# The triangular inverse on two diagonal 64x64 blocks, with part of its transposes on VectorE

## What is computed

```python
a_mat = jnp.einsum('bhncd,bhnsd->bhncs', kb, k) * decay * strict
m_mat = jnp.eye(chunk, dtype=jnp.float32) + a_mat
rhs = jnp.concatenate([vb, kb * jnp.exp(gc)[..., None]], axis=-1)
sol = lax.linalg.triangular_solve(m_mat, rhs, left_side=True, lower=True, unit_diagonal=True)
u_c, w_c = sol[..., :DV], sol[..., DV:]
```

## Time and profile before

| | |
|---|---|
| time, median of 3 runs | 1202.3 us (1195.59, 1203.81, 1202.3) |
| profiled execution, span | 1200.4 us |
| TensorE busy | 1187.7 us (99%) |
| VectorE busy | 790.3 us (66%) |
| ScalarE busy | 523.0 us (44%) |
| DMA | 99.69 MB, mean 83 GB/s |
| mean granted TensorE clock | 0.993 |

### The profile page before, as it was taken

One profiled execution on the slowest core, in us unless ns is written; L12 is line 12 of the kernel. 1 busy time (PEld: TensorE's weight loads), 2 busy tenths in 40 slices (PEclk: granted clock), 3 DMA queues, 4 the chain that ended last, 5 costly groups with the idle time before them and its releaser, 6 DMA issues.

```text
span 1200.4 us, 20994 instructions
## 1 busy us (share of the span) xinstructions
PE 1187.7 (99%) x8792; PEld 1162.9 (97%) x8792; DVE 790.3 (66%) x1153; ACT 523.0 (44%) x841; POOL 63.3 (5%) x48
## 2 busy tenths in 40 slices
PE   9999999999999999999999999999999999999997
PEld 9999999999999998999999897999999999999997
DVE  6887565767566733766665787547776667675764
ACT  6445343435345532433553454443354344354355
POOL 0000000000000300000104100220000000000003
PEclk9999999999999999999998999999999999999999
DMA  5322212222212332152300002422133121223112
GB/s 191 129 85 75 105 63 97 89 98 78 106 72 106 106 106 70 55 71 71 111 1 2 1 1 88 132 77 83 54 126 120 63 97 63 97 106 106 71 71 79
DMA packets 39213, 99.69 MB, mean 83 GB/s; under 512 B 12112, under 2 KB 15568, under 8 KB 39120
## 3 DMA queue, kind: packets, MB, share of 16 engines
q1 hardware_dynamic: 38064, 96.00, 24.0%
q10 hardware_dynamic: 1056, 2.36, 0.5%
HBM read 92.91 MB, written 5.44 MB: 82 GB/s over the span
## 4 chain that ended last, share of the span: by engine, by line
PE 95%; DVE 2%; ACT 1%; issue 1%; POOLq 0%; DVEq 0%; POOL 0%
PE ps L857 34%; PE ps L824 21%; PE ps L773 20%; PE ps L969 11%; PE ps L1361 4%; PE ps L737 1%; PE ps L1167 1%; PE ps L1375 1%; ACT x_hi L1443 1%; DVE w_lo L1950 1%; DVE h L2012 1%; PE ps L928 0%; PE ps L939 0%; PE ps L993 0%; PE ps L1273 0%
## 5 line engine op out<-in xcount | busy, mean ns | idle before, releaser
L857 PE MATMUL ps<-x_hi,s_hi 128*128 128x296 f32 (+1 forms) x576 | 171.5, 298 | 0.2
L857 PE MATMUL ps<-x_hi,s_lo 128*128 128x296 f32 (+1 forms) x576 | 171.0, 297 | 0.0
L857 PE MATMUL ps<-x_lo,s_hi 128*128 128x296 f32 (+1 forms) x576 | 170.7, 296 | 0.0
L773 PE MATMUL ps<-x_hi,w_hi 128*128 128x296 f32 (+1 forms) x608 | 135.8, 304 | 0.2 <-DVE x_lo L1955 0.2
L773 PE MATMUL ps<-x_lo,w_hi 128*128 128x296 f32 (+1 forms) x608 | 132.0, 298 | 0.0
L773 PE MATMUL ps<-x_hi,w_lo 128*128 128x296 f32 (+1 forms) x608 | 131.8, 298 | 0.0
L857 PE MATMUL ps<-t_hi,s_hi 128*128 128x296 f32 (+1 forms) x432 | 128.5, 297 | 0.0
L857 PE MATMUL ps<-t_hi,s_lo 128*128 128x296 f32 (+1 forms) x432 | 128.3, 297 | 0.0
L857 PE MATMUL ps<-t_lo,s_hi 128*128 128x296 f32 (+1 forms) x432 | 128.1, 296 | 0.0
L2049 DVE TENSOR_TENSOR s_lo<-s_sum,s_hi 128x1024 fp32r<-128x1024 f32 x72 | 88.2, 1225 | 44.1 <-ACT s_hi L1430 41.4
L857 PEld LDWEIGHTS ps<-x_hi,s_hi 128*128 128x128 f32 x576 | 108.5, 188 | 0.6 <-issue 0.6
(11 more groups left out here) (325 smaller groups left out, 2554.8 us busy)
## 6 DMA issues: line engine op xcount, KB each, us to landing
raw<-weights SPq DMA_DIRECT2D x150, 512.0 KB, 3.4
raw<-weights SPq DMA_DIRECT2D x16, 384.0 KB, 3.5
S<-states SPq DMA_DIRECT2D x1, 2048.0 KB, 10.5
new_state<-S ACTq DMA_DIRECT2D x1, 2048.0 KB, 6.8
y_t<-h SPq DMA_DIRECT2D x4, 336.0 KB, 2.3
h<-x_t SPq DMA_DIRECT2D x4, 296.0 KB, 4.6
h<-x_t SPq DMA_DIRECT2D x2, 592.0 KB, 7.4
raw<-weights SPq DMA_DIRECT2D x4, 256.0 KB, 5.2
```

Source lines behind the costliest of these rows:

```text
L773: last = nc.tensor.matmul(ps[:, slot if out is None else out, half, 0:w_half], w[:, slot, k, :], x[:, k, a:a + w_half], start=(k == 0 and ...
L857: last = nc.tensor.matmul(out, w[:, k, :], x[:, k, :], start=(start and k == 0 and r == 0), stop=(k == KT // 2 - 1 and r == 2), skip_group ...
```

## The change

For tiles 1 to 4 the levels 1 to 5 never leave the two 64x64 blocks on the diagonal. The change holds just these two blocks, one in partitions 0 to 63 and one in partitions 64 to 127, side by side in 64 columns (`x_small`, `y_small` in plane 0, `t_small`). A product of 128x128 becomes two of 64x64: rows 0 to 63 into partitions 0 to 63, and rows 64 to 127 into partitions 64 to 127 (`DIAGONAL`). VectorE's masks and subtractions of these levels have half the columns. Up to level 4 the blocks to be turned are 32x32 or smaller, so for the levels 0 to 4 X is made from Y by VectorE's own transpose of 32x32 blocks (`V.transpose`), and TensorE's transposes and ScalarE's copies of these levels are gone. After level 5, TensorE turns one 64x64 block per head and ScalarE copies it; the subtraction of level 5 is two instructions that write into the full Y. The subtraction of level 6 becomes a multiplication by -1. A wait of the old first transposes (`att_ready`, `y_ready`, `u_ready`) moves to `low` of level 1, q = 1. Tile 0 keeps its steps. The mask table is 128 columns narrower. `ORDER` is unchanged. The core of the diff:

```diff
@@ -244,10 +245,13 @@
 MASK = {}
 _at = 0
 for _n, _w in (("ident", P), ("incl", P), ("neg", P), ("incl4", P), ("neg4", P), ("same4", P),
-               ("levels", 7 * P), ("group", NG)):
+               ("levels", 4 * MAIN), ("ident64", HALF_P), ("levels64", 6 * HALF_P), ("group", NG)):
+
+DIAGONAL = (slice(0, HALF_P), slice(HALF_P, P))
...
@@ -263,11 +267,17 @@
     m[:, MASK["incl4"]] = (s <= c) & same
     m[:, MASK["neg4"]] = np.where((s <= c) & same, 0.0, -1e30)
     m[:, MASK["same4"]] = same
-    for l in range(7):
+    for l in range(6):
         w = 1 << l
-        a = MASK["levels"].start + l * P
         block = (s // (2 * w) == c // (2 * w)) & (s % (2 * w) < w) & (c % (2 * w) >= w)
-        m[:, a:a + P] = block.T if l else block
+        block = block.T if l else block
+        if l < 4:
+            a = MASK["levels"].start + l * MAIN
+            m[:, a:a + MAIN] = block[:, 0:MAIN]
+        a = MASK["levels64"].start + l * HALF_P
+        for r in DIAGONAL:
+            m[r, a:a + HALF_P] = block[r, r]
+    m[:, MASK["ident64"]] = s % HALF_P == c[:, 0:HALF_P]
...
@@ -484,6 +494,29 @@
         def half_bank(j, half, n):
             return bank(j).rearrange("p (x h c) -> p x h c", x=2, h=2)[0:n, half, :, 0:n]
 
+        def half_small(j, half):
+            return bank(j).rearrange("p (x h c) -> p x h c", x=2, h=2)[:, half, :, 0:HALF_P]
+
+        def x_small(t):
+            return XY[t % 2][:, 0, :, 0:HALF_P]
+
+        def y_small(t):
+            return XY[t % 2][:, 0, :, HALF_P:P]
+
+        def t_small(t):
+            return T1[t % 2][:, :, 0:HALF_P]
+
+        def two_heads(ap, q):
+            return ap[:, 2 * q:2 * q + 2]
+
+        def first_mask(l):
+            a = MASK["levels"].start + l * MAIN
+            return mask[0:MAIN, a:a + MAIN]
+
+        def small_mask(l):
+            a = MASK["levels64"].start + l * HALF_P
+            return mask[:, a:a + HALF_P]
...
@@ -1146,17 +1179,12 @@
                     for hd in range(H):
                         last = mm(heads(a, n)[0:n, hd, :], kv[:, hd, cols], kv[:, hd, cols])
                     last.then_inc(s["kk_ps"], 1)
-                else:
+                elif t == 0:
 
                     pe.wait_ge(s["y_first"][p], t // 2 + 1)
                     for q in range(2):
                         if q == 1:
-                            if t < 2:
-                                pe.wait_ge(s["att_ready"], t + 1)
-                            elif t == 2:
-                                pe.wait_ge(s["y_ready"][0][1], LEVELS[0] - 1)
-                            else:
-                                pe.wait_ge(s["u_ready"], t - 2)
+                            pe.wait_ge(s["att_ready"], t + 1)
                         turned(t, q)
 
             def turned(t, q):
@@ -1164,7 +1192,11 @@
                 n = TILES[t][1]
                 p, a, b, base = chain_at(t)
                 for hd in range(2):
-                    last = nc.tensor.transpose(half_bank(a + q, 0, n)[:, hd, :], inverse(t)[:, 2 * q + hd, 0:n], m("ident", n))
+                    if t == 0:
+                        last = nc.tensor.transpose(half_bank(a + q, 0, n)[:, hd, :], inverse(t)[:, 2 * q + hd, 0:n], m("ident", n))
+                    else:
+                        r = DIAGONAL[0]
+                        last = nc.tensor.transpose(half_small(a + q, 0)[r, hd, :], inverse(t)[r, 2 * q + hd, r], ident[r, r])
                 last.then_inc(s["x_ps"][p][q], 1)
             def low(t, lq):
@@ -1173,10 +1205,20 @@
                 n = TILES[t][1]
                 p, a, b, base = chain_at(t)
                 pe.wait_ge(s["x_ready"][p][q], base + l)
+                if t and l == 1 and q == 1:
+                    if t == 1:
+                        pe.wait_ge(s["att_ready"], t + 1)
+                    elif t == 2:
+                        pe.wait_ge(s["y_ready"][0][1], LEVELS[0] - 1)
+                    else:
+                        pe.wait_ge(s["u_ready"], t - 2)
                 for hd in range(2 * q, 2 * q + 2):
                     if l == 6:
                         last = mm(half_bank(a + q, 0, n)[HALF_P:P, hd - 2 * q, 0:HALF_P], AT[p][0:HALF_P, hd, HALF_P:P],
                                   XY[p][0:HALF_P, 0, hd, 0:HALF_P])
+                    elif t:
+                        for r in DIAGONAL:
+                            last = mm(half_small(a + q, 0)[r, hd - 2 * q, :], AT[p][r, hd, r], x_small(t)[r, hd, :])
                     else:
                         last = mm(half_bank(a + q, 0, n)[:, hd - 2 * q, :], AT[p][0:n, hd, 0:n], XY[p][0:n, 0, hd, 0:n])
                 last.then_inc(s["t1_ps"][p][q], 1)
@@ -1191,6 +1233,9 @@
                     if l == 6:
                         last = mm(half_bank(a + q, 1, n)[0:HALF_P, hd - 2 * q, HALF_P:P], T1[p][HALF_P:P, hd, 0:HALF_P],
                                   inverse(t)[HALF_P:P, hd, HALF_P:P])
+                    elif t:
+                        for r in DIAGONAL:
+                            last = mm(half_small(a + q, 1)[r, hd - 2 * q, :], t_small(t)[r, hd, :], y_small(t)[r, hd, :])
                     else:
                         last = mm(half_bank(a + q, 1, n)[:, hd - 2 * q, :], T1[p][0:n, hd, 0:n], inverse(t)[:, hd, 0:n])
                 last.then_inc(s["p_ps"][p][q], 1)
@@ -1199,6 +1244,8 @@
 
                 l, q = lq
                 p, a, b, base = chain_at(t)
+                if t and l < 5:
+                    return
                 pe.wait_ge(s["y_ready"][p][q], base + l)
                 turned(t, q)
...
@@ -1778,18 +1825,23 @@
             def start(t, i):
                 n = TILES[t][1]
                 p, a, b, base = chain_at(t)
-                if i == 1:
+                if i == 1 and t == 0:
                     for q in range(2):
                         turned(t, 0, q)
 
             def turned(t, l, q):
                 n = TILES[t][1]
                 p, a, b, base = chain_at(t)
-                act.wait_ge(s["x_ps"][p][q], base + l + 1)
-                nc.scalar.copy(pair(XY[p][:, 0], q, n), half_bank(a + q, 0, n)).then_inc(s["x_ready"][p][q], 1)
+                act.wait_ge(s["x_ps"][p][q], l + 1 if t == 0 else FLIPS[t])
+                if t:
+                    r = DIAGONAL[0]
+                    nc.scalar.copy(two_heads(x_small(t), q)[r], half_small(a + q, 0)[r]).then_inc(s["x_ready"][p][q], 1)
+                else:
+                    nc.scalar.copy(pair(XY[p][:, 0], q, n), half_bank(a + q, 0, n)).then_inc(s["x_ready"][p][q], 1)
 
             def flip(t, lq):
-                turned(t, *lq)
+                if t == 0 or lq[0] == 5:
+                    turned(t, *lq)
...
@@ -2456,19 +2508,46 @@
                 n = TILES[t][1]
                 p, a, b, base = chain_at(t)
                 if i:
+                    if t:
+                        for q in range(2):
+                            turned(t, 0, q)
                     return
                 dve.wait_ge(s["kk_ps"], t + 1)
                 dve.wait_ge(s["e_ready"], t + 1)
                 V.tensor_tensor(AT[p][0:n, :, 0:n], heads(a, n)[0:n], E_[p][0:n, :, 0:n], ALU.mult).then_inc(s["at_ready"], 1)
                 dve.wait_ge(s["at_ready"], t + 1)
 
-                link(V.tensor_tensor(T1[p][0:n, :, 0:n], AT[p][0:n, :, 0:n], over_heads(m("levels", n, 0), n), ALU.mult))
+                if t:
+                    for r in DIAGONAL:
+                        last = V.tensor_tensor(t_small(t)[r], AT[p][r, :, r], small_mask(0)[r].unsqueeze(1).to_broadcast([HALF_P, H, HALF_P]),
+                                               ALU.mult)
+                    link(last)
+                else:
+                    link(V.tensor_tensor(T1[p][0:n, :, 0:n], AT[p][0:n, :, 0:n], over_heads(first_mask(0), n), ALU.mult))
                 if t == 2:
                     dve.wait_ge(s["neg_vn_ps"], 1)
                 if t > 2:
                     dve.wait_ge(s["u_ps"], t - 2)
-                V.tensor_tensor(inverse(t)[:, :, 0:n], over_heads(m("ident", n), n), T1[p][0:n, :, 0:n],
-                                ALU.subtract).then_inc(s["y_first"][p], 1)
+                if t == 1 or t == 2:
+                    V.memset(inverse(t)[HALF_P:P, :, 0:HALF_P], 0.0)
+                if t:
+                    V.tensor_tensor(y_small(t), over_heads(mask[:, MASK["ident64"]], P), t_small(t),
+                                    ALU.subtract).then_inc(s["y_first"][p], 1)
+                else:
+                    V.tensor_tensor(inverse(t)[:, :, 0:n], over_heads(m("ident", n), n), T1[p][0:n, :, 0:n],
+                                    ALU.subtract).then_inc(s["y_first"][p], 1)
+
+            def turned(t, l, q):
+                p, a, b, base = chain_at(t)
+                if l == 0:
+                    dve.wait_ge(s["y_first"][p], t // 2 + 1)
+                else:
+                    dve.wait_ge(s["y_ready"][p][q], base + l)
```

(21 more changed lines are left out.)

3 lines of the change are left out of this document (2 added, 1 removed).

## The result

| | before | after |
|---|---|---|
| time, median (range) of 22 runs each | 1201.9 us (1195.55 to 1203.91) | 1205.72 us (1202.02 to 1211.84) |
| after over before, 95% interval | | 1.005 (1.0035 to 1.0065) |
| span of the profiled execution | 1200.4 us | 1203.9 us |
| mean granted clock of that execution | 0.993 | 0.982 |

The change makes the kernel 0.5% slower, under the 1% that I called the limit of what a measurement tells; the forecast was 0.9% faster.

The account below looks back on a forecast made before the run. TensorE was taken as the bound (95% of the span), VectorE next. Of 21.7 us off TensorE's list, 15.4 could count at best; less 4.4 for waits, gain 11: span 1189.4, median 1191 us, 8-in-10 range 1184 to 1206.

Parts of the forecast that it names:

- TensorE's list: TensorE's work in the gated-delta stage: 46.2 us of records go, 24.5 come, so 21.7 us shorter.
- The price of a pair: Two 64x64 block records on TensorE, run side by side, cost 0.0575 us together; 320 pairs make 18.4 us.
- The rival of blocks that do not overlap: In long runs each 64x64 record costs 0.0575 us; TensorE's list only 3.3 us shorter, 1198 to 1201; chance 0.15.
- VectorE's sum over the stage: Masks and subtractions get shorter, 40 transposes add 11.2 us: +3 us used, bounds -4 and +9.
- The rival of dear transposes: VectorE's transposes cost double, 0.56 us: 11 us more, VectorE the bound everywhere, gain 4, 1198; chance 0.08.
- Meshing: From 640 to 740 us both in-order engines, over 80% full, would not mesh perfectly: 4.4 us charged, 1 per 20.
- the bound by the fuller engine: Larger of TensorE's and VectorE's busy time per stretch, 640 to 740 us: 85.6 us, at most 14.4 gained there.
- The place was the one named: At the scan's step, state updates and an output operation precede two transposes: a new 1.5 us wait, up to three times.
- The clock: Granted clock, half speed from 626 to 640 us before the change; no added half clock was charged in the forecast.
- an extension: Half clock lasting past 640 us: without a slower kernel chance 0.07, slower by over 1% chance 0.10.
- held on to 660 us: Clock rival's case of half clock lasting from 626 to 660 us: costs up to 10 us, no gain, 1202.
- the good half: Part of the forecast 1186 to 1197 counted as under 1190.3, faster by over 1%: 0.23 of its chance 0.43.

Follow-up runs that it names:

- e3: Changed kernel, 16-column state products of the last two of four heads streamed wider; median 1205.4 us, ratio 1.005; its profiled execution was among three at 1196.2 to 1198.6.
- e2: Kernel before, with its 16-column state products streamed over all columns from the group's first to the tile's 80th; 1195.6 us, ratio 0.9968.
- e9: e5 with the first product (low) of every level 1 to 5 of tiles 1 to 4 streamed over 128 columns; 1192.2 us, ratio 0.9943.
- e5: Changed kernel with state products widened and each VectorE transpose put directly behind the subtraction that makes its Y; 1194.8 us, ratio 0.9957.
- e10: e8 with VectorE's transposes put back at the flip's own later place in the order; 1196.6 us, ratio 0.9974.
- e8: e5 with the first product (low) of tile 1 and of tile 2's levels 1 and 2 streamed over 128 columns; 1190.5 us, ratio 0.9921.

## Why the prediction was wrong, step by step

**TensorE's list: right, 2 us short.** Between before and the profiled e3, at the same clock in the stage, TensorE's busy time falls from 133.73 to 113.90, 19.8 us; the sum said 21.7. Between e2 and e9, both at full clock, it falls by 10.9, and the 160 wider pairs of e9 were put at 8 us: 18.9. The price of a pair holds over long runs. From e5, at full clock, in order of time:

```profile
708.21 0.68 PE L1002 MATMUL ps<-d_inv,d_t 64*64 64x64 f32 x16
708.73 0.63 PE L1002 MATMUL ps<-d_inv,d_a_t 64*64 64x64 f32 x16
```

Sixteen records, eight pairs, in 0.52 us: 0.065 a pair: the first pair of a run takes 0.05 more, the others the 0.0575 of the sum. The rival of blocks that do not overlap is out. The Trainium skill (TensorE: Matmul & The Clock Gate, What happens when you issue a matmul) gives about 62 ns per matmul where the sequencer's software decodes it. By the rows it is 0.52 / 16 = 0.033 us per record here, so that figure does not hold for this kernel. The Trainium skill (TensorEngine Tiling, Restrictions and Gotchas) says that a column-tiled array has no transpose mode for fp32 input. Here the 16 transposes of 64x64 blocks at L1199 are 16 records, not the 32 of full products; whether the array was column-tiled for them, no run tells.

**VectorE: prices right, sum 4 us too high.** By form, 600 to 780 us of after:

```profile
L2546 DVE STREAM_TRANSPOSE d_inv<-d_inv 128x128 f32<-128x128 f32 x40 | 10.8, 292 | 0.1
L2561 DVE TENSOR_TENSOR d_t<-ps,mask 128x128 f32<-128x128 f32 x40 | 10.7, 284 | 8.1 <-PE ps L1002 7.8
```

A transpose takes 292 ns (0.28 taken), a mask 284 (0.28). VectorE's sum over the stage goes from 100.71 to 99.64, where I had +3, well within the bounds. The rival of dear transposes is out.

**Meshing (how far both engines stay busy at once): the right mechanism, mis-sized.** I charged 4.4 us for it, on top of the bound by the fuller engine. Taken together, 21.7 us off the list and 11 off the time meant 10.7 us more of idle TensorE. In e3 against before it is 16.96 - 3.13 = 13.8 us, and the stage is 6.0 us shorter, not 11. The missing 5 us are 3.1 of idle time and 1.9 of the list. The place was the one named, behind the scan step, but the wait there was 2.24 us and not 1.5: the cast L2678, another 0.75 us, stands between the output operation and the transposes. And the same wait arises behind other work, ten times in all, not three. What these waits cost is known from e10 against e8: the place of the transposes is 3.5 us.

**The clock: the step that failed.** The term that I put at nothing in the sum is what the lighter list does to the granted clock: I kept the 14 us at half clock of before and gave an extension only 0.17 in all. It was 37.5 us in the profiled execution, 625.4 to 659.6 and 724.4 to 727.8, against 13.6 before. The 23.9 us more, at 0.38 each, are 9.1 us. Busy time in the stage says it in another way: the list that shrinks by 19.8 us at equal clock shrinks by only 133.73 - 125.60 = 8.1 in after, and the idle time rises by 14.78 - 3.13 = 11.7; the difference is the 3.5 us lost. My rival of "held on to 660 us" named 10 us and 1202; with the 5 us of the other step it is nearly what came. What makes the clock fall and come back is not shown by any run; what it costs is. What I held against it, that level 6 and the waits of 734 to 740 had passed at full clock, was evidence from single runs of 64x64 records inside dense work, not from 20 us made of them. And it was wrong to take the half clock of before as a fixed part of the kernel: half of its executions do not have it.

The forecast of 11 us of gain is thus missed by 5 us of waits and list and about 9 to 9.5 of clock: 11 - 5 - 9.5 = -3.5. That 1205.7 still lies within the range of 1184 to 1206 is luck: two losses came together there, where each rival had one. One slip beside it: under 1190.3 lie 4.3 of the 11 us of the forecast's width, which is less than the good half that I counted as faster by over 1%.

## What to carry to other kernels

Where TensorE is full and the change takes columns from it, ask what the clock will do with the lighter list before adding up records: here a kernel with less work for TensorE was slower, and one with more (e8 against e5) faster. Where a small operation that TensorE waits for moves to an in-order engine that is over 80% full, put it directly behind the operation that makes its input; its old place in the order was chosen for another engine. Compare kernels at equal granted clock, by execution, before a few tenths of a percent are put down to anything else.

## What the runs showed of the hardware

- The kernel before runs in two ways, 1195.9 and 1202.2 us (medians of the 65 and the 71), by whether the granted clock falls: 13.6 us at 1.2 GHz cost 6.3 us, 0.46 for each. In the changed kernel, which waits more, each cost an estimated 0.38 (6.4 us for 17 between executions of 0.987 and 0.980).
- With the state products widened, the kernel before kept its clock in all 12 executions (0.997 or more), at no price that can be seen: its stage at full clock is 6.3 us shorter than that of before with the fall, 130.59 against 136.86.
- Two 64x64 blocks on the diagonal of the array run side by side over 32 records in a row without coming apart (e5, from 708.21), 0.005 to 0.007 us between the two of a pair and, behind the first pair, 0.057 to 0.060 from pair to pair.
- The place of the transposes on VectorE sets TensorE's waits for them: 10.1 us behind the scan's operations and 3.1 directly behind the subtractions (e10 and e8), at the same granted clock.
- TensorE's busy time hides part of a wait: a 64x64 record is shown as 0.22 us long where the next could start after 0.0575, so each gap is an estimated 0.16 us longer than it is shown.
